# Gated linear attention in a two-layer pair of blocks: outputs by rows, both directions as pairs on halves of TensorE, gates of two heads beside the projections

## What is computed

```python
b = jnp.cumsum(log_a.astype(jnp.float32).reshape(B, n, C, H, dk), axis=2)
b_mid = b[:, :, C // 2:C // 2 + 1]
b_last = b[:, :, -1]
qc = q * jnp.exp(b - b_mid)
kc = k * jnp.exp(b_mid - b)
A = jnp.einsum('bnihd,bnjhd->bnhij', qc, kc)
...
intra = jnp.einsum('bnhij,bnjhe->bnihe', A, v)
k_dec = k * jnp.exp(b_last[:, :, None] - b)
chunk_state = jnp.einsum('bnjhd,bnjhe->bnhde', k_dec, v)
...
inter = jnp.einsum('bnihd,bnhde->bnihe', q * jnp.exp(b), S_prev)
...
o = _rmsnorm(o_f + o_b, out_norm)
return jax.nn.silu(gr) * o.reshape(B, S, H * GLA_DV)
```

## Time and profile before

| | us |
|---|---|
| timed runs (3) | 2877.33, 2887.67, 2892.20; median 2887.67 |
| profiled execution | 2878.68, its span 2876.8 |
| projections of `w_odd_v` (857.07 to 957.31) | 100.24 |
| recurrence, heads 0 to 3 (957.31 to 1111.85) | 154.54 |
| from the last inter matmul to the first of `w_out_odd` | 14.03 |

### The profile page before, as it was taken

The page is one execution under the profiler, slowest core; times in us unless marked ns, Lnnn a source line. Parts: engine busy times, 40 slices in busy tenths (PEclk is TensorE's granted clock), DMA queues, the critical chain, the costliest instruction groups (busy, mean ns, idle before and its releaser), DMA issues. The chain is left out here.

```text
span 2876.8 us, 29534 instructions
## 1 busy us (share of the span) xinstructions
PE 2476.7 (86%) x11630; PEld 1182.0 (41%) x11630; DVE 1252.8 (44%) x2412; ACT 1304.4 (45%) x2135; POOL 298.0 (10%) x347
## 2 busy tenths in 40 slices
PE   5989989998989988899899888787994989887993
PEld 1334734443434654344344356443331334343331
DVE  3455644545344353454544645424213543524212
ACT  5645556656566334566656434531114464321113
POOL 0000000000001130000000520001231101101131
PEclk8999999999999767999999876788997999887997
DMA  4220012221232000123123110325983220125995
GB/s 164 73 90 0 1 59 88 88 99 65 100 112 88 30 1 30 59 89 117 61 93 141 44 49 12 156 80 213 411 341 120 88 88 30 78 99 193 394 416 211
DMA packets 67755, 335.90 MB, mean 117 GB/s; under 512 B 12008, under 2 KB 12040, under 8 KB 53408
## 3 DMA queue, kind: packets, MB, share of 16 engines
q1 hardware_dynamic: 50448, 266.11, 24.4%
q0 software_dynamic: 17168, 67.90, 6.2%
HBM read 370.64 MB, written 23.07 MB: 137 GB/s over the span
## 5 line engine op out<-in xcount | busy, mean ns | idle before, releaser
L359 PE MATMUL PB<-AS,WS 128*128 128x512 f16 x1544 | 597.0, 387 | 98.2 <-DVE AS L424 37.1
L360 PE MATMUL PB<-AS,WS 128*128 128x512 f16 x1544 | 597.3, 387 | 0.0
L361 PE MATMUL PB<-AS,WS 128*128 128x512 f16 x1544 | 595.7, 386 | 0.0
L309 DVE SCALAR_TENSOR_TENSOR WS<-raw,sc,WS 128x1024 f16<-128x1024 f32 (+3 forms) x288 | 328.0, 1200 | 102.3 <-ACT WS L298 102.3
L298 ACT ACTIVATE WS<-raw,sc 128x1024 f16<-128x1024 f32 (+3 forms) x288 | 283.5, 1055 | 74.4 <-DVE sc L275 74.4
L359 PEld LDWEIGHTS PB<-AS,WS 128*128 128x128 f16 x1544 | 152.5, 99 | 322.2 <-issue 79.0
L255 ACT ACTIVATE junk<-raw 128x1024 f16<-128x1024 f32 (+3 forms) x288 | 280.6, 974 | 9.3
L2690 PE MATMUL PB<-T 128*64 128x512 f32 x768 | 234.3, 613 | 11.4 <-issue 8.7
L361 PEld LDWEIGHTS PB<-AS,WS 128*128 128x128 f16 x1544 | 153.5, 99 | 190.0 <-issue 13.9
L360 PEld LDWEIGHTS PB<-AS,WS 128*128 128x128 f16 x1544 | 152.7, 99 | 184.7 <-issue 17.3
L284 DVE TENSOR_REDUCE sc<-sc 128x1 f32<-128x4 f32 x72 | 11.3, 157 | 414.1 <-POOL sc L263 414.1
(11 more groups left out here) (552 smaller groups left out, 3721.1 us busy)
## 6 DMA issues: line engine op xcount, KB each, us to landing
T<-in_moe_up SPq DMA_DIRECT2D x26, 2048.0 KB, 10.7
raw<-in_w_up SPq DMA_DIRECT2D x22, 2048.0 KB, 7.9
T<-in_moe_down SPq DMA_DIRECT2D x26, 1024.0 KB, 13.2
raw<-in_w_down SPq DMA_DIRECT2D x16, 1408.0 KB, 6.0
raw<-in_w_in_even SPq DMA_DIRECT2D x9, 2048.0 KB, 8.0
raw<-in_w_in_odd SPq DMA_DIRECT2D x8, 2048.0 KB, 7.7
moe_y<-X SPq DMA_DIRECT2D x32, 512.0 KB, 10.4
WS<-in_moe_up SPq DMA_DIRECT2D x6, 2048.0 KB, 15.2
```

Source lines behind the costliest of these rows:

```text
L309: e.scalar_tensor_tensor(lo[q], raw[q], s, hi[q], MUL, SUB).then_inc(*k.s("dve_split").up("lo", i, q))
L359: e.matmul(bank, wh[:, q, c, :], act.hi[c], start=c == 0, stop=False)
L360: e.matmul(bank, wh[:, q, c, :], act.lo[c], start=False, stop=False)
L361: m = e.matmul(bank, wl[:, q, c, :], act.hi[c], start=False, stop=c == kt - 1)
```

## The change

The outputs now have tokens on partitions: in `intra` the masked A is the weight and 256 values stream, in `inter` 64 columns of q are the weight and the 256 state values stream, and each direction writes the 64 partitions of its chunk. Since d = 0 handles chunk n and d = 1 chunk 7 - n, one is even and one odd, so the two `state` matmuls stand on different 64-row halves and the two `inter` matmuls on different 64-column halves; they are issued next to each other. For heads 2 and 3 the states alternate between two pairs of banks. The norm's sum is now along the free axis (ACT Square with accumulator), ACT scales rows, and PE turns the head back with eight transposes (`back`), after which DVE multiplies once. Both directions add into one `at`. `kd` and `qb` are no longer exponentials of ACT but products on POOL with columns `el` and `em` broadcast over 64; DVE's `z` (the bias) and `far` are gone, and Abs reads the bank. `go(2)` now stands behind each of the 16 tiles, for the gates of heads 0 and 1; those of heads 2 and 3 stand in the recurrence of heads 0 and 1.

```diff
-GLA_STATE = (2, 5)
+def gla_state(h, n, d):
+
+    return ((2, 5) if h < 2 or n % 2 == 0 else (0, 1))[d]
+def gla_state_past(h, n):
+
+    back = 1 if h < 2 else 2
+    return (h, n - back) if n >= back else (h - 1, 6 if n == 0 else 5)
...
 def gate_banks(h):
 
-    return (4, 5, 6) if h == 0 else (0, 0, 1)
+    return (4, 5, 6) if h < 2 else (0, 0, 1)
...
+    steps = iter([(h, s, d) for h in range(2) for s in range(8) for d in range(2)])
...
             if d == 1:
-                w.wait_ge(*v.past("z", h, 0))
+                w.wait_ge(*a.past("abs", h, 0))
...
             pe_rows(k, e, w, "w_odd_v", 4 * n, q, act, PB[q][:, :], False)
-            if n == 1:
-                go(1)
+            go(2)
...
+        for q in (1, 2, 0, 3):
+            x = e.matmul(gla_out(k, h, q), m.at[h % 2][:, 128 * q:128 * q + 128], m.gv[:, q, 256 * h:256 * h + 256], start=q < 2,
+                         stop=False, skip_group_check=True)
...
+    def state(h, n):
+
+        for d in range(2):
+            w.wait_ge(*a.past("kdn", h, d))
...
+                w.wait_ge(*v.past("S", *gla_state_past(h, n), d))
+        for d in range(2):
+            c = n if d == 0 else 7 - n
+            r0, q = 64 * (c % 2), c // 2
+            e.matmul(PB[gla_state(h, n, d)][:, 0:256], m.kc[h][d][r0:r0 + 64, 128 * q:128 * q + 128],
+                     m.gv[r0:r0 + 64, q, 256 * h:256 * h + 256], start=True, stop=True, skip_group_check=True).then_inc(
+                *p.up("state", h, n, d))
+
+    def inter(h, n):
+
+        for d in range(2):
+            w.wait_ge(*v.past("S", h, n - 1, d))
+            w.wait_ge(*g.past("qb", h, d))
+        for d in range(2):
+            c = n if d == 0 else 7 - n
+            r0, q = 64 * (c % 2), c // 2
+            e.matmul(gla_out(k, h, q)[r0:r0 + 64, :], m.qb[h][d][:, 64 * c:64 * c + 64], m.sst[d][(n + 1) % 2], start=False,
+                     stop=False, skip_group_check=True).then_inc(*p.up("inter", h, n, d))
+
+    def back(h):
+        w.wait_ge(*a.past("on", h, 3))
...
+            if h < 2:
+                gate(h + 2, n, 0)
+                gate(h + 2, n, 1)
+            if h > 0 and n == 4:
+                back(h - 1)
+    back(3)
...
             if h >= 2:
-                w.wait_ge(*p.past("inter", h - 2, 7, d))
-            e.activation(m.qb[j][d], m.ax[d], ACT.Exp, scale=1.0 / 16).then_inc(*a.up("qb", h, d))
...
+                w.wait_ge(*g.past("qb", h - 2, d))
+                w.wait_ge(*v.past("S", h - 2, 6, d))
+            for what, out, src, at in (("dec", m.dec, m.ax, last), ("em", m.em, m.ax, mid), ("el", m.el, m.bb, last)):
...
+    def normed_rows(h):
+        w.wait_ge(*p.past("inter", h, 7, 1))
+        row_squares(h, (0, 3))
...
+        for q in range(4):
+            e.activation(m.on[:, 256 * q:256 * q + 256], gla_out(k, h, q), ACT.Copy, scale=m.ss[h % 2][:, q:q + 1]).then_inc(
+                *a.up("on", h, q))
...
+        if h > 0:
+            normed_rows(h - 1)
...
+            e.tensor_scalar(m.qc[d], PB[zb][:, :], k.col("gb_f" if d == 0 else "gb_b", h), 0.0, ADD, MIN).then_inc(
+                *v.up("min", h, d))
```

More of the change, by code:

```diff
@@ L1470, in gla_total @@
         for i in range(2):
-            w.wait_ge(*a.past("square", "head", h, i))
-            x = e.matmul(PB[1][:, :], k.cst("ones"), k.h[2 * h + i], start=i == 0, stop=i == 1)
-        x.then_inc(*p.up("gla_total", h))
+            for q in range(4):
+                o = 256 * q + 128 * i
+                x = e.transpose(gla_back(k, h, i)[:, 128 * q:128 * q + 128], m.on[:, o:o + 128], k.cst("ident"))
+            x.then_inc(*p.up("back", h, i))
     for h in range(4):
-        j, banks = h % 2, gla_out_bank(h)
@@ L1477, in odd0_pe @@
[L1477 to L1495, removed]
@@ L1496, in odd0_pe @@
-        for n in range(8):
[L1497 to L1521, removed]
@@ L1522, in odd0_pe @@
-    gla_total(3)
+        intra(h)
+        for n in range(8):
+            if n < 7:
+                state(h, n)
+            if n > 0:
+                inter(h, n)
+            if h < 2:
[4 more added lines that the diff above has]
+    back(3)
     def free(bank):
@@ L1598, in odd0_act @@
     for h in range(4):
+        if h > 0:
+            normed_rows(h - 1)
         for n in range(8):
[L1600 to L1604, removed]
+            if h < 2:
+                gate(h + 2, n, 0)
+                gate(h + 2, n, 1)
             if h > 0 and n == 6:
                 head_sum(h - 1)
[L1607 to L1610, removed]
+        w.wait_ge(*p.past("inter", h, 5, 1))
+        row_squares(h, (1, 2))
+    normed_rows(3)
     head_sum(3)
-    w.wait_ge(*p.past("gla_total", 3))
     act_parts(k, e, w, "odd0", "mix", H, k.as_hi)
@@ L1624, in gate @@
         zb, ab, _ = gate_banks(h)
-        j = h % 2
-        b3, last, mid = by64(m.ax[d]), 63 if d == 0 else 0, 32 if d == 0 else 31
+        b3, mid = by64(m.ax[d]), 32 if d == 0 else 31
         if s == 0:
@@ L1639, in gate @@
             w.wait_ge(*g.past("chunk"))
+            if h:
+                w.wait_ge(*p.past("T", h - 1, d))
             e.tensor_tensor(m.bb[d], m.qc[d], m.ax[d], SUB).then_inc(*v.up("gate", h, d))
@@ L1704, in odd0_dve @@
                         w.wait_ge(*p.past("inter", h, n - 1, d))
[L1705 to L1709 removed]
+                    e.scalar_tensor_tensor(new, old, m.dec[h % 2][d][:, c:c + 1], ps, MUL, ADD).then_inc(*v.up("S", h, n, d))
+            if h < 2:
+                gate(h + 2, n, 0)
+                gate(h + 2, n, 1)
+            if h > 0 and n in (4, 5):
+                head_out(h - 1, n - 4)
     for i in range(2):
```

171 lines of the change are left out of this document (92 added, 79 removed).

## The result

The changed kernel takes 2836.02 us (median of 4 runs, 2832.33 to 2842.8) where the kernel before takes 2883.51 (2877.33 to 2892.2, 4 runs): ratio 0.9836, 95% interval 0.9801 to 0.9871. That is 1.6% faster, clear of the noise. The forecast was 2845, within 2808 to 2877. The profiled execution is the slowest of the four, 2842.8.

A forecast was written before the change was run, and what follows sets the result against it. PE was taken to bound the recurrence, much of it at 1.2 GHz. Projections +14.2, recurrence -49.8 and norm -1.3 give -36.9 against 2878.7: 2842, put at 2845 because the runs' median lies higher; range 2808 to 2877.

The forecast's parts named there:

- Pairs: Recurrence: a pair of states or inters costs about one state before; a step 1.2 or 2.2 us, for 2.43 or 4.38.
- the rival that halves do not overlap: Recurrence: states and inters drain into each other, a step at 1.2 GHz is 4.4 us again; total 2895; chance 0.1.
- Change of tiling: Each recurrence step changes tiling mode twice, about 0.2 us a change: step 1.25 us for 0.85, 6 us over 14 steps.
- Heads 2 and 3 at 17 each: Recurrence without gates: 11.4 us a head at the high clock, 20.8 at the low one; 17 each taken.
- the first rival (11.4 each): Clock stays up: heads 2 and 3 take 11.4 us each, heads 0 and 1 some 8 less each; about 2817; chance 0.2.
- The lower bound of 10: Heads 2 and 3 of the recurrence: 10 us if switching between row and column halves costs nothing.
- Heads 0 and 1: Recurrence with gates: 33.7 and 37 us for 40.11 and 44.58; waits for S of step 3, norm ahead of Abs.
- ACT's `dec` behind DVE: Heads 0 and 1: ACT's `dec` of head 2 waits for S of step 6, at 24.2 us, because columns are shared.
- The items I listed up to DVE's difference: Head 0's gate chain from intra on: states, z, minimum, Abs, Exp, table loads and Ln, summed as 10.1 us.
- Projections: Two gates instead of one: 93.8 us of PE work, 17.2 of stall, 3.5 of lower clock; 114.5 for 100.24, +14.2.
- The 8.72 us of the earlier trace: Projections: PE's stall ahead of head 0's second A goes, since A now stands at a chunk's third tile.
- Norm: Head norm at the end of the stage: 12.7 us for 14.03, -1.3.

The follow-up runs named there:

- 2.8 us in each head for the columns: Changed kernel with own places for the columns `dec`, `em` and `el` of all four heads: 2830.45 us (1 run).
- 2.2 for the norm: Changed kernel with the norm of head 0 moved behind the first two gate steps of head 3: 2832.53 us (1 run).
- the two kernels of the same projections with the better clock: Two follow-up kernels whose projections do not differ from the changed kernel's: projections 115.34 and 115.37 us, for 118.26 in the changed kernel.
- the two short executions: Profiled executions of two follow-up kernels with the changed kernel's projections, where the high clock held longer: projections 115.34 and 115.37 us.
- the banks alone: Changed kernel with separate banks for each direction's z, A and T of a gate, POOL as it was: 2819.74 us (1 run).
- both together: Changed kernel with DVE doing the gate products of heads 0 and 1, plus banks per direction: 2804.18 us (1 run).
- 10.2 us once the stalls were out: Changed kernel with DVE's products, own columns, later norm and banks per direction: 2795.57 us; the same remedies with gates in their old place: 2810.24 us.

## Why the prediction was right, and where it was off

- **Pairs.** Right. Each pair cost what one matmul did, a step 1.22 us for the 1.2 forecast. Pairs taken apart cost 32.7 us; the rival that halves do not overlap is excluded. The profile of before had such a pair already, the two states of step 0, four records in the time of two:

```profile
1087.93 0.70 PE L1508 MATMUL PB<-T,AS 64*128 64x256 f32 x4
1089.14 0.70 PE L1508 MATMUL PB<-T,AS 64*128 64x256 f32 x2 [0.51 <-DVE AS L1699]
```

- **Change of tiling.** I took 0.2 us a change from the earlier trace rows, so 0.85 + 2 x 0.2 for a step. The changed kernel shows it directly: 0.43 us for a pair of states behind another pair of states, 0.63 for one behind an inter, 0.58 for a pair of inters behind a state. That a change of tiling drains the engine is the rule of the Trainium skill, TensorEngine Tiling (Array Packing), Tiling Modes, Key Properties. This trace agrees with it: 0.15 to 0.20 us a change.
- **Heads 2 and 3 at 17 each.** Mis-sized: 12.48 and 12.57, at a granted clock of 1.00. I split the difference between the clocks; the first rival (11.4 each) was right on the clock for these two heads, and short by about 1.1 us. Those are PE's waits for DVE's updates (12.48 - 11.29 = 1.19), which I had put beside the next pair. The lower bound of 10 does not follow from my own figures either: 1.8 + 7 x 0.85 + 1.2 is 9.0.
- **Heads 0 and 1.** 33.53 and 37.35 for 33.7 and 37, with the waits where I put them: S of step 3 (5.55 us for 7), ACT's `dec` behind DVE (9.51), the norm ahead of Abs. The runs put both of the last on the path: 2.8 us in each head for the columns, 2.2 for the norm. That the numbers fit so well is in part luck. The items I listed up to DVE's difference add up to 11.8 us and not to the 10.1 I wrote; it began 11.5 us after intra, and DVE's part took 6.1 and not 7.2. And the granted clock is 0.69 and 0.68, not near 0.5. In the sentence on what bounds the kernel, DVE is not under half in head 2 of before: 21.85 of 42.26 us.
- **Projections.** Mis-sized: +18.0 for +14.2, though +15.1 in the two kernels of the same projections with the better clock. The waits on POOL were 3.94 and 4.31 (4.4 and 4.5 forecast), those of z 1.56 and 1.96 (1.5 and 1.7), the second A 0.91 and 0.98 where I had 1.6 and 1.7, T 0.92 each: 15.5 in all, less than my 17.2. PE's work at the high clock is 92.3 and not 93.8. What I had too small is the clock: PE's busy time is 102.75, and 92.30 with no stall, so the stalls cost 10.4 us of lower clock (7.4 in the two short executions) and not 3.5. A behind a stall takes 1.5 to 2.1 us, and the f16 tile behind the z of 920.51 goes on at 0.63 a record until 926.
- **Cause of those stalls.** POOL's switch for the first A, as I wrote: with the products on DVE the wait is gone. What I had not priced is how the rest hangs on shared banks, 10.6 us in the projections. The 8.72 us of the earlier trace rows went with the new order as forecast (0.91 and 0.98 ahead of the second A).
- **Norm.** -1.1 for -1.3.
- **Sum.** Two errors of size, 9.0 us too much for heads 2 and 3 (34 - 25.05) and 3.8 too little for the projections, partly cancel; that the total fits better than its terms is luck. The stage moved by -41.7 and the profiled executions by -35.8 (2876.8 to 2841.0): some is lost where the change touches nothing, as in a stretch with the same 784 matmul records that took 142.00 us before and 146.20 after. The medians moved by -47.5; the profiled execution lies low among the runs before (2878.68) and is the highest after (2842.8).

## What to carry to other kernels

Matmuls that fill half of the array belong next to their partners in the queue: the order of issue alone was worth 33 to 46 us here. Price a stall of TensorE with the clock behind it: 9.0 us of waits took 6.4 more with them. And where one engine is named as the releaser, look at what else is queued there at that time, and at what a remedy adds to another engine's queue: moving the products away from POOL alone showed 2.3 us, since DVE's queue and a shared bank held the next matmul, the banks alone showed 10.6, and both together 26.0. The placement of the gates showed no gain as made, and 10.2 us once the stalls were out. So a remedy or a placement that shows nothing alone is not yet refuted.

## What the runs showed of the hardware

- Two f32 matmuls on different halves, issued next to each other, took the time of one (84 records, 19.3 us busy); with one of another tiling between them they took 39.5.
- A pair behind a change of tiling took 0.15 to 0.20 us more than a pair behind its like (0.63 and 0.58 for 0.43).
- POOL stood still for 6.66 to 7.25 us between a partition sum and the first multiplication, ten times in five kernels, as 14.3 for two in the earlier trace rows. In three more it was 8.23 or 8.24, and there the stretch ended with ACT's exponentials.
- POOL's products with a column broadcast over 64 values took 1.04 us, the plain ones 1.25 to 1.35 (both in the projections); I had taken 1.7 for the former, from the earlier trace rows.
- The granted clock is not read off PE's busy share: 0.57 with PE busy for 38.64 of 43.48 us (head 0, pairs apart), 0.69 with 23.56 of 33.53 (head 0, paired), 1.00 with 18.42 of 18.50 (head 2, pairs apart) and with 11.29 of 12.48 (head 2, paired). What decides it stays open.
